# A memory stage whose vector list, roots and copies change engine and order, in a two-layer hybrid decoder on Trainium2

## The reference

```
qk    = (q @ k.T) * exp(logD - m)                 # "decays" times scores
num   = qk @ v + a_inter * (q @ C);  nq likewise with n
h     = num / max(|nq|, exp(-m))
C_new = a_c * C + (k*w).T @ v
out_m = h * rsqrt(mean(h*h over the head) + eps) * g * sigmoid(gate)
```

## Time and profile before

| | |
|---|---|
| three runs | 1849.45, 1852.46, 1852.45 us, median 1852.45 |
| the profiled execution | 1849.23 us, span 1847.0 us |
| busy share of the span | PE 91%, DVE 52%, ACT 38%, POOL 21% |
| chain that ended last, by engine | PE 81%, DVE 7%, POOL 4%, issue 3%, ACT 2%, DMA 1% |
| memory stage of layer 0, first DVE instruction to first matmul of the output projection | 274.77 to 351.72 us |
| the same in layer 1 | 1059.55 to 1132.58 us |

### The profile page before, as it was taken

How to read it: one execution, slowest core, us unless ns; L and a number is a source line. 1 busy time by engine, 2 the same in 40 slices (tenths; PEclk the granted TensorE clock), 3 DMA queues, 4 the chain that set the end, 5 groups by cost and what they waited for, 6 DMA issues and landing times.

```text
span 1847.0 us, 33779 instructions
## 1 busy us (share of the span) xinstructions
PE 1687.7 (91%) x13514; PEld 1625.7 (88%) x13514; DVE 954.0 (52%) x1433; ACT 696.2 (38%) x1050; POOL 391.3 (21%) x236
## 2 busy tenths in 40 slices
PE   6999978799999999998999877859999999999993
PEld 5999857789999999998998567859999999999993
DVE  5577676532210122226776765255746548457474
ACT  4533363342221223235333633443534435335342
POOL 4300250343443344443002503030000000000031
PEclk8999986699999999999999877969999999999997
DMA  4222227422222223222222212368778678677682
GB/s 176 81 70 77 74 72 266 188 80 92 92 87 86 81 92 105 79 81 69 69 77 78 70 50 86 112 211 277 241 246 288 217 255 290 216 266 259 234 313 75
DMA packets 71225, 271.42 MB, mean 147 GB/s; under 512 B 11668, under 2 KB 12404, under 8 KB 70300
## 3 DMA queue, kind: packets, MB, share of 16 engines
q1 hardware_dynamic: 63988, 250.52, 39.7%
q10 hardware_dynamic: 3464, 10.62, 1.8%
q0 software_dynamic: 3648, 8.53, 1.3%
HBM read 253.24 MB, written 36.34 MB: 157 GB/s over the span
## 4 chain that ended last, share of the span: by engine, by line
PE 81%; DVE 7%; POOL 4%; issue 3%; ACT 2%; DMA 1%; ACTq 0%; DVEq 0%; POOLq 0%; SPq 0%
PE psum L1189 39%; PE psum L1709 11%; PE psum L1719 10%; PE psum L1711 9%; PE psum L1236 9%; POOL r_cvt L674 2%; POOL r_w L676 1%; PE psum L1688 1%; PE psum L1241 1%; PE psum L1677 1%; DVE n L1780 1%; POOL r_cvt L675 1%; DVE r_bt L1964 0%; DVE acc L1767 0%; DMA wraw<-in_w_in 0%
## 5 line engine op out<-in xcount | busy, mean ns | idle before, releaser
L1709 PE MATMUL psum<-xg,xhi 128*128 128x320 f32 x1408 | 371.4, 307 | 1.2 <-issue 0.9
L1711 PE MATMUL psum<-xg,xlo 128*128 128x256 f32 x1408 | 369.7, 282 | 0.0
L637 POOL TENSOR_TENSOR wlo<-wraw,whi 128x1024 fp32r<-128x1024 f32 (+1 forms) x90 | 231.3, 2572 | 405.0 <-ACT whi L777 405.0
L1709 PEld LDWEIGHTS psum<-xg,xhi 128*128 128x128 f32 x1408 | 265.2, 188 | 3.5 <-issue 3.1
L1711 PEld LDWEIGHTS psum<-xg,xlo 128*128 128x128 f32 x1408 | 265.3, 188 | 0.0
L1189 PE MATMUL psum<-xnh,whi 128*128 128x260 f32 x1120 | 234.6, 291 | 32.1 <-POOL xnl L694 12.5
L777 ACT CAST whi<-wraw 128x1024 fp32r<-128x1024 f32 (+1 forms) x130 | 140.7, 1085 | 288.4 <-DMA wraw<-in_w_in 161.9
L415 DVE TENSOR_TENSOR xlo<-xraw,xhi 128x1024 fp32r<-128x1024 f32 x176 | 215.2, 1224 | 54.3 <-ACT xhi L1137 54.2
L1137 ACT CAST xhi<-xraw 128x1024 fp32r<-128x1024 f32 x176 | 182.7, 1048 | 142.1 <-PE psum L1711 142.0
L1189 PE MATMUL psum<-xnl,whi 128*128 128x260 f32 x1120 | 228.3, 286 | 0.0
L1189 PE MATMUL psum<-xnh,wlo 128*128 128x260 f32 x1120 | 228.2, 286 | 0.0
(11 more groups left out here) (427 smaller groups left out, 2422.1 us busy)
## 6 DMA issues: line engine op xcount, KB each, us to landing
xraw<-in_moe_gu SPq DMA_DIRECT2D x176, 512.0 KB, 4.2
xraw<-in_moe_dn SPq DMA_DIRECT2D x64, 704.0 KB, 5.8
wraw<-in_w_in SPq DMA_DIRECT2D x54, 512.0 KB, 3.2
wraw<-in_ffn_gu SPq DMA_DIRECT2D x44, 512.0 KB, 3.2
wraw<-in_ffn_dn SPq DMA_DIRECT2D x16, 704.0 KB, 4.1
wraw<-in_w_out SPq DMA_DIRECT2D x16, 512.0 KB, 3.5
out_cache_s<-in_cache SPq DMA_DIRECT2D x4, 2040.0 KB
rows_in<-in_zero SPq DMA_DIRECT2D x8, 640.0 KB, 33.8
```

The costliest lines, as they stand in the source:

```text
L637: pool.tensor_tensor(wlo[u % RAW][:, 0:cols], wraw[u % RAW][:, 0:cols], whi[u % SPL][:, 0:cols].bitcast(F32), ALU.subtract).then_inc(lo_ma ...
L1709: pe.matmul(epart(n), xhi[n % HIX][:, k * P:(k + 1) * P], xg[:, k, :], start=(k == 0), stop=False, skip_group_check=True)
L1711: ins = pe.matmul(epart(n)[:, 0:256], xlo[n % RWX][:, k * P:(k + 1) * P], xg[:, k, 0:256], start=False, stop=(k == KD - 1), skip_group_che ...
```

## The change

1. DVE's list: `weighted_keys(0)`, `(1)` and the last pass over S8 go ahead of the first `running`; `decayed(0)` and `(1)` come between the chunk states; after `c8_update` come `decayed(2)`, `(3)`, and only then `finish(0)`; the later calls are shuffled; `obs` and `normalise(4)` move ahead of `wv`, and a `split_lo` of unit 0 of `w_out` is put in.
2. `dw` and `qd` get other places, so ACT's wait for `decode_made` 2 goes.
3. The four short roots of each layer, the router's root and the last roots are made by POOL as a multiply-add and a power with exponent -0.5. The last roots are made tile by tile.
4. The six state DMAs go from ACT's queue, after the last gate, to SP's queue, once `mt` 2 is made. There they stand behind the caches and zeros in layer 0, and before the loads of units 3 to 7.
5. All eight `xnl` are made by DVE. POOL makes fewer low parts of `w_out` ahead of them: unit 0 goes to DVE, and in layer 0 unit 2 waits for all `xnl`.
6. `wv` goes behind `mt` 3 and has two matmuls a sample (one over 80 partitions with four columns) instead of three.

```diff
@@ SP
+                    if n == RAW - 1:
+                        made(sp, li, "mt", 2)
+                        for name, src in (("hgrn_p", R["sall"][:, NC - 1, :, :]), ("mlstm_p", R["call"][:, NC, :, :]),
+                                          ("hgrn_s", flat(TQ, 3 * NB * 64)), ("mlstm_s", flat(TSV, 3 * NB * 65)),
+                                          ("m_p", proj[0:5, 5, SEQ - 1:SEQ]), ("m_s", R["sc8"][0:5, 32:40])):
+                            sp.dma_start(a[name][li], src).then_inc(S("state_out"), 16)
@@ POOL, mlstm stage
+                for k, ss in enumerate((R["ss2"][:, 0:NC], R["ss2"][:], R["s10"][:], R["ss2"][:])):
+                    pool.wait_ge(S("ob_ms"), 4 * li + k + 1)
+                    step(pool.tensor_scalar(ss, ss, 1.0 / 64, EPS, ALU.mult, ALU.add))
+                    bump(pool.tensor_tensor(ss, ss, nhalf[0:ss.shape[0], 0:ss.shape[1]], ALU.pow), S("ob_rms"), pool)
                 if li == 0:
-                    for n in range(SPL):
-                        lo(U_OUT[0] + n, KD * P)
+                    pool.wait_ge(lo_made, los(U_OUT[0]) + 1)
+                    lo(U_OUT[0] + 1, KD * P)
+                    pool.wait_ge(mixl_dve, KD)
+                    lo(U_OUT[0] + 2, KD * P)
                 else:
-                    split_lo(pool, U_OUT[1], KD * P, lo_pool)
-                for m in range(0, KD, 2):
-                    pool.wait_ge(mixh_made, KD * li + m + 1)
...
+                    split_lo(pool, U_OUT[1] + 1, KD * P, lo_pool)
@@ POOL, router and end
+            pool.wait_ge(S("squares_added"), 1)
+            step(pool.tensor_scalar(rms[:], rms[:], 1.0 / D, EPS, ALU.mult, ALU.add))
+            bump(pool.tensor_tensor(rms[:], rms[:], nhalf[:, 0:5], ALU.pow), S("rms_ready"), pool)
...
+            for t in range(5):
+                r = rms[0:tok(t), t:t + 1]
+                pool.wait_ge(S("last_squares"), t + 1)
+                step(pool.tensor_scalar(r, r, 1.0 / D, EPS, ALU.mult, ALU.add))
+                bump(pool.tensor_tensor(r, r, nhalf[0:tok(t), 0:1], ALU.pow), S("last_rms"), pool)
@@ ACT, mlstm
-                act.wait_ge(S("decode_made"), 3 * li + 2)
...
                 made(act, li, "mo", 4)
-                for n in range(SPL):
+                hi(U_OUT[li], KD * P)
+                act.wait_ge(S("ob_ms"), 4 * li + 4)
+                for n in range(1, SPL):
                     hi(U_OUT[li] + n, KD * P)
@@ DVE, mlstm
-                sig(tt(S8, S8, vb, ALU.add), "decode_made")
...
-                decayed(0)
-                decayed(1)
                 weighted_keys(0)
                 weighted_keys(1)
+                sig(tt(S8, S8, vb, ALU.add), "decode_made")
                 running(0)
                 weighted_keys(2)
+                decayed(0)
                 running(1)
                 weighted_keys(3)
+                decayed(1)
                 running(2)
                 running(3)
                 s8_out()
                 c8_update()
+                made(v, li, "mo", 0)
+                decayed(2)
+                made(v, li, "mo", 1)
+                decayed(3)
                 finish(0)
+                finish(1)
                 mean_squares(li, 2)
-                finish(1)
-                decayed(2)
-                decayed(3)
+                finish(2)
                 normalise(li, 2)
-                finish(2)
-                mean_squares(li, 3)
                 finish(3)
                 decayed(4)
+                mean_squares(li, 3)
+                gate_heads(li, 2)
                 normalise(li, 3)
-                gate_heads(li, 2)
                 c8_out()
                 finish(4)
                 mean_squares(li, 4)
+                gate_heads(li, 3)
+                v.wait_ge(S("ob_rms"), 4 * li + 3)
+                sig(tt(R["obs"][:], R["obs"][:], bc(R["s10"][:].unsqueeze(2), NB, 10, 64), ALU.mult), "obs_normed")
+                split_lo(v, U_OUT[li], KD * P, lo_dve if li else lo_made)
+                normalise(li, 4)
                 made(v, li, "wv")
...
-                gate_heads(li, 3)
-                v.wait_ge(S("obs_rms"), li + 1)
-                sig(tt(R["obs"][:], R["obs"][:], bc(R["s10"][:].unsqueeze(2), NB, 10, 64), ALU.mult), "obs_normed")
-                normalise(li, 4)
                 made(v, li, "fx")
...
-                for m in range(1, KD, 2):
+                for m in range(KD):
                     v.wait_ge(mixh_made, KD * li + m + 1)
                     tt(xnl[:, m, :], proj[:, MIXT[m], :], xnh[:, m, :].bitcast(F32), ALU.subtract).then_inc(mixl_dve, 1)
```

More of the change, by code:

```diff
@@ L707, in _ @@
                             norm_lo(2, m)
-            for n in range(2, KD, 2):
+            pool.wait_ge(mixl_dve, 2 * KD)
+            for n in range(3, KD, 2):
                 split_lo(pool, U_OUT[1] + n, KD * P, lo_pool)
+            pool.wait_ge(S("squares_added"), 1)
+            step(pool.tensor_scalar(rms[:], rms[:], 1.0 / D, EPS, ALU.mult, ALU.add))
+            bump(pool.tensor_tensor(rms[:], rms[:], nhalf[:, 0:5], ALU.pow), S("rms_ready"), pool)
             pool.wait_ge(cleared, 128)
@@ L1535, in outputs, with values @@
                         for c in range(NC):
-                            j.mm(c * 65, 65, R["qd"][:, h % 2, c * P:(c + 1) * P], R["va"][:, c, h, :])
+                            j.mm(c * 65, 65, qd[h % 2][:, c * P:(c + 1) * P], R["va"][:, c, h, :])
                         j.end()
+                def values():
+                    pe.wait_ge(state_in, 64 * (li + 1))
+                    j = Job(li, "wv")
+                    own = spw[0:80, 64:96].rearrange("p (g c) -> p g c", g=2)
+                    for b in range(NB):
+                        c = 2 * b
+                        j.mm(c, 2, R["cv"][:, b, 0, :], spw[:, c:c + 2])
+                        j.last = pe.matmul(j.out(16, 32).rearrange("p (g c) -> p g c", g=2)[:, :, c:c + 2],
+                                           R["cv"][0:80, b, 1, :], own[:, :, c:c + 2], start=True, stop=True,
+                                           skip_group_check=True)
+                    j.end()
                 taken(pe, li, "mq", 2, 3)
@@ L1567, in mlstm @@
                 outputs((4,))
-                pe.wait_ge(state_in, 64 * (li + 1))
-                j = Job(li, "wv")
-                for b in range(NB):
-                    c = 2 * b
-                    j.mm(c, 2, R["cv"][:, b, 0, :], spw[:, c:c + 2])
-                    for g, (r, rows) in ((1, (0, 64)), (2, (64, 16))):
-                        j.mm(16 * g + c, 2, R["cv"][r:r + rows, b, 1, :], spw[r:r + rows, 64 + c:66 + c])
-                j.end()
                 turn_heads(li, 3)
+                values()
                 pe.wait_ge(S("obs_normed"), li + 1)
@@ L2293, in _ @@
                 for n in range(KD):
[L2294 removed]
+                    if li and n % 2 == 0 and n + 2 < KD:
                         split_lo(v, U_OUT[1] + n + 2, KD * P, lo_dve)
```

68 lines of the change are left out of this document (27 added, 41 removed).

## The result

The changed kernel takes 1840.85 us (median of four runs, 1839.31 to 1842.71) against 1851.5 for the kernel before in the same session (1849.45 to 1852.46): a ratio of 0.9948, with a 95% interval of 0.9932 to 0.9964. The sign was right; the size lies outside the range of 1812 to 1838. Its profiled execution took 1840.13 us with a span of 1838.3, against 1849.23 and 1847.0 before.

A forecast was written before the change was run, and what follows sets the result against it. PE's matmuls were taken as the bound, with time to win only where PE stands still: 14.6 - 0.4 + 5.6 + 0.85 + 4.4 = 25 us off 1849.23 gives 1824.2, plus 0.8: 1825 us, range 1812 to 1838.

The forecast's parts named there:

- Layer 0: Memory stage and output projection of layer 0: same edits gain 5.6 us of 15, as DMAs set another end.
- the stop behind unit 2: Layer 0's output projection: PE stands 8 to 12 us, unit 3's weights being queued behind zero fills.
- rival A: Layer 0: SP's queue doesn't hold back the loads, gain some 16 us instead of 5.6, about 1814; chance 0.12.
- Layer 1: Layer 1's memory stage: reordered work starts the output projection earlier, gain 14.6 us, less 0.4 for powers.
- B: Layer 1's tail: PE at half clock sets the end and DVE waits 5 us, about 1830; chance 0.11.
- The collision: Layer 1's tail: POOL's low part of unit 1 delays DVE's `normalise(4)`, adding 2.4 us; bounds 0 and 2.5.
- A pair of powers: Multiply-add and power on POOL replacing ACT's roots: taken as 2.0 us a pair, between 0.9 and 3.0.
- C: POOL's power is long: no gain at 4.7 us a pair, 1866 us in all at 6; chance 0.08.
- The router: Router's root on ACT replaced by a POOL pair: gain 0.85 us with a pair up to 2.3.
- the sum itself: Whole kernel: the terms add to 25 us off the profiled execution's 1849.23 us.
- the term for the end: Kernel's end: with last roots made tile by tile, DVE's first scaling starts at once, gain 4.4 us.
- D: Output projections: what the tails win is lost to another wait, no measurable change, 1850 us; chance 0.05.

The follow-up runs named there:

- g4_pool_later: Changed kernel with GpSimd's low part of unit 1 in layer 1 put behind the seventh low part of the mixed rows: 1837.62 us, ratio 0.9944.
- e1_pad: Kernel before with 128 unused bytes of SBUF behind `spw`, so later tiles lie where the changed kernel has them: 1854.91 us, ratio 1.0027.
- e2_addr: Changed kernel with `spw`, `st8` and `nhalf` placed so that every later tile has its old address: 1832.94 us, ratio 0.9919.
- f3_code: Changed kernel with eight `wv` matmuls repeated idly in layer 0, putting the feed-forward loop at its old program place: 1836.77 us, ratio 0.9946.
- f4_end_two: Changed kernel with VectorE's flag reading and jump ahead of the last additions, and two pairs of last powers instead of five: 1838.75 us, ratio 0.9948.
- h3_best: Changed kernel with old addresses and loop place, zeros in layer 1, early jump, two power pairs and GpSimd's unit 1 low part later: 1814.33 us, 0.9809.
- h2_three: Changed kernel with old addresses, the loop's old place, early jump and two power pairs; zeros stay in layer 0: 1825.14 us, ratio 0.9865.
- e4_branch_early: Changed kernel with VectorE's flag reading and jump over the second pass put ahead of the last five additions: 1839.74 us, ratio 0.9945.
- g3_copies_act: Changed kernel with the six state copies issued by ScalarE again, ahead of its casts: 1846.18 us, ratio 0.9990.

## Why the prediction was wrong

**What held.** Layer 0: 5.5 us for 5.6, with the stop behind unit 2 where it was placed, so rival A falls. Layer 1: 13.3 us of stage for 14.2; `wv` set no end (DVE does not wait behind it), so B falls. The collision: 2.15 for 2.4, by g4_pool_later. A pair of powers 1.2 to 2.2 for 2.0, so C falls. The router 1.1 for 0.85.

**The first step that failed** is the sum itself: "14.6 - 0.4 + 5.6 + 0.85 + 4.4 = 25 us off the profiled execution's own 1849.23". It takes every stretch without an edit as unchanged. But the diff also moved addresses (64 bytes in `spw`, 64 in `nhalf`) and shortened a straight piece of TensorE's program ahead of a loop; the prediction counted the removed matmuls for the time they take and named the shift of the experts' addresses nowhere. Together they cost 10.1 us by the ledger: 6.4 in the experts, shown from both sides by e1_pad and e2_addr, and 3.7 in FF, of which the stop and the clock's fall behind it are shown by f3_code. This is 10.1 of the 16.3 us between the 25 forecast and the 8.7 of the ledger.

**The second** is the term for the end: "tile by tile the first can start at once, at 1833.9: gain 4.4". The 4.41 us named ACT as releaser, and the step did not ask what stood right behind. There were two more: DVE's own flag and jump, 0.9 + 2.8 us under ACT's roots, and GpSimd's powers locking out DVE's scalings, the same collision that the prediction had priced in layer 1 and did not look for here. The gain was 0.2, so 4.2 us are missing here; with both mended it is 1.4 to 2.8 in the four runs that have this (25.9 in f4_end_two to 27.3 in h3_best, against 28.7). In f4_end_two the scalings still wait 1.5 us for the first pair of powers, which "at once" had put at nothing.

**Smaller sizes.** The rest of the distance, some 2 us, is layer 1: 0.9 in the stage itself and 1.2 in the attention ahead of it, whose length varied from run to run.

**D**, that nothing measurable happens because a win is lost to a late load, was not it: layer 1's win stayed, and the losses are of other kinds. That h2_three comes to 1825 does not make every term exact: against the forecast its end gave 2.6 us less, layers 0 and 1 0.6 less each, and the experts, which were to stay as they were, 1.7 more. No further loss of that size is missing.

## What to carry to other kernels

Read a diff for what it moves as well: addresses behind a grown tile and the place of a loop behind removed instructions; here they took back 10 of some 19 us won. Pad so that hot tiles keep their addresses, or try 128 bytes either way on its own before judging a change. Where a wait goes, list everything under it up to the next instruction, the sequencer's loads and jumps and the other engine on the shared port among them.

## What the runs showed of the hardware

- 128 bytes of SBUF address cost TensorE 3% of a high-part matmul (303 to 312 ns) and the program 5 to 6 us, with no instruction changed (e1_pad).
- Behind a jump over a long block DVE's next instruction came 2.8 us later, though the branch itself took 63 ns; with the jump put ahead, the wait was gone (e4_branch_early).
- A loop's place in TensorE's program, eight matmuls earlier, cost a stop of 2.3 us and, with the clock, some 5 us of that stretch (f3_code).
- On ACT's queue, beside SP's fills and cache copies, the last of six copies (1.74 MB in all) landed 24.5 us behind its issue: the other queue alone did not get them past (g3_copies_act).
- A GpSimd multiply-add of 0.19 us took up to 1.28 beside VectorE's scalings of 1.2 (e4_branch_early).
